# A decoder trunk on one core: loads, remainders and waits reordered at the start, at gate and up, and at the per-layer gate

## The reference

```
h = rmsnorm(x, norm_mix[i]);  proj = h @ w_in            # the indexer's columns first, in layer 0
x = x + mixer(proj) @ w_out[i]
h = rmsnorm(x, norm_ffn[i])
x = x + (gelu(dwconv(h @ w_gate[i])) * (h @ w_up[i])) @ w_down[i]
gate = sigmoid(rmsnorm(x, norm_ple[i]) @ w_ple_gate[i])
x = x + gate * (p[i] @ w_ple_proj[i])
```

## Time and profile before

| | |
|---|---|
| median of 3 runs | 3091.38 us (3091.03 to 3097.04) |
| the profiled execution | 3092.02 us, its span 3090.1 us |
| mean granted TensorE clock | 0.991 |
| PE busy | 2984.3 us, 97% of the span, 14830 matmuls |
| PE busy, tenths of the first four of 40 slices (77 us each) | 7, 9, 9, 9 |
| DVE, ACT, POOL busy | 73%, 47%, 34% |
| DMA | 349.07 MB moved, mean 113 GB/s |

### The profile page before, as it was taken

One profiled execution on the slowest core, in us unless ns is written; L12 is line 12 of the kernel. 1 busy time (PEld: TensorE's weight loads), 2 busy tenths in 40 slices (PEclk: granted clock), 3 DMA queues, 4 the chain that ended last, 5 costly groups with the idle time before them and its releaser, 6 DMA issues. The chain is left out here.

```text
span 3090.1 us, 44240 instructions
## 1 busy us (share of the span) xinstructions
PE 2984.3 (97%) x14830; PEld 2499.8 (81%) x14830; DVE 2255.3 (73%) x3681; ACT 1443.5 (47%) x3127; POOL 1059.7 (34%) x689
## 2 busy tenths in 40 slices
PE   7999999999999999999989999999999999999989
PEld 6778887988878888888868888899887888888867
DVE  5599987889378888888743341899548888879852
ACT  4385536878243334344522211888534333344531
POOL 3105445465223323201122645677323333310120
PEclk9999999999999999999999999999999999999999
DMA  5323334222314563476211694333122222276411
GB/s 175 128 58 99 96 127 108 50 56 68 130 61 150 157 157 101 147 248 194 79 48 41 215 199 147 87 68 75 48 90 72 82 82 82 82 261 216 136 48 48
DMA packets 288086, 349.07 MB, mean 113 GB/s; under 512 B 88316, under 2 KB 181292, under 8 KB 287916
## 3 DMA queue, kind: packets, MB, share of 16 engines
...
...
## 5 line engine op out<-in xcount | busy, mean ns | idle before, releaser
L2188 DVE TENSOR_SCALAR_CACHE_REDUCE k_x<-k_x,l0in_cand,l0in_want 128x384 bf16<-128x384 f32 (+1 forms) x186 | 175.0, 1004 | 1.2 <-DVE l0in_before L2183 0.2
L78 PE MATMUL l1in_acc<-k_w_lo,k_hi 128*128 128x512 f32 x384 | 151.0, 393 | 4.2 <-PEq L99 2.4
L80 PE MATMUL l1in_acc<-k_w_hi,k_hi 128*128 128x512 f32 x384 | 150.0, 391 | 0.0
L79 PE MATMUL l1in_acc<-k_w_hi,k_lo 128*128 128x512 f32 x384 | 149.9, 390 | 0.0
L2567 ACT ACTIVATE k_x<-k_x 128x512 f32<-128x512 f32 x88 | 55.6, 632 | 185.6 <-DVE k_x L2773 180.9
L725 DVE TENSOR_TENSOR l1in_sq<-l1in_out 128x512 f32<-128x512 f32 x32 | 41.3, 1291 | 111.4 <-ACT l1in_out L658 110.6
L1649 DVE TENSOR_TENSOR l1dil_pt_lo<-l1dil_ring,l1dil_pt_hi 128x512 fp32r<-128x512 f32 x192 | 101.9, 553 | 4.6 <-ACT l1dil_pt_hi L1585 2.3
L1585 ACT ACTIVATE l1dil_pt_hi<-l1dil_ring 128x512 fp32r<-128x512 f32 x192 | 92.4, 492 | 22.7 <-PE l1dil_ring L1732 21.4
L1665 DVE CUSTOM_DVE_ANT_0 l1dil_s<-l1dil_s,l1mix_sliding 128x128 f32<-128x128 f32 (+7 forms) x128 | 97.2, 761 | 7.4 <-PE l1dil_s L1749 2.2
L2665 POOL TENSOR_TENSOR l1ff_raw_g<-l1ff_raw_g 128x512 f32<-128x512 f32 x10 | 12.9, 1291 | 243.4 <-DVE l1ff_w_lo L2729 243.4
L2665 POOL TENSOR_TENSOR l0ff_raw_g<-l0ff_raw_g 128x512 f32<-128x512 f32 x10 | 12.9, 1292 | 231.2 <-DVE l0ff_w_lo L2729 231.2
...
## 6 DMA issues: line engine op xcount, KB each, us to landing
...
k_raw<-in_w_in_odd SPq DMA_DIRECT2D x24, 512.0 KB, 4.9
...
```

The costliest lines, as they stand in the source:

```text
L78: pe.matmul(out, a_hi, b_lo, start=start, stop=False)
L79: pe.matmul(out, a_lo, b_hi, start=False, stop=False)
L80: return pe.matmul(out, a_hi, b_hi, start=False, stop=stop)
L2188: tick(dve.tensor_scalar(hits[:, cols], score[:, cols], cand[:, i:i + 1].bitcast(F32), want[:, i:i + 1], ALU.is_ge, ALU.add, accum_out=exc ...
```

## The change

In the first stage, chunks 2 and 3 get a buffer of their own, `early`, laid over a part of `w_lo` that is written only later (second strip); so four chunks are in flight. The norm weights are copied second instead of third. The four remainders of the first strip are made by DVE and no longer by POOL, which waits for them before its later work. ACT takes the squares of tile 1 behind `split(1)`, and `round(1)` and the squares of tile 2 behind `split(3)`. PE turns tile 1 in the middle of unit 0. In the per-layer gate, `p`'s second half is issued behind the second chunk instead of behind the fifth. In gate and up, PE's steps of the first three pieces wait for nothing (POOL gave them their counts before), tile 7 is scaled between the two sums, POOL's first addition waits until it is scaled, and piece 5 is split and finished before the second sums.

```diff
+        early_in = [st.sem(f"early_in{b}") for b in range(2)]
+        early = st.sb("early", [P, 2 * kc, 512], at=low_at + KD * 512 * 4)
...
             def load(n):
                 s, c = n // CH, n % CH
-                if n >= 2:
-                    sp.wait_ge(lo_ready, n - 1)
+                if n >= 4:
+                    sp.wait_ge(lo_ready, n - 1 if n >= 6 else n - 3)
...
             load_x(0)
+            feed.load(sp)
             sp.dma_start(square[:], square_src).then_inc(square_in, 16)
-            feed.load(sp)
             load(0)
+            load(1)
             load_x(1)
-            load(1)
+            load(2)
+            load(3)
             for t in range(2, 4):
                 load_x(t)
...
             square(0)
-            square(1)
             split(0)
             feed.round(act, 0)
             split(1)
+            square(1)
+            split(2)
+            split(3)
+            feed.round(act, 1)
             square(2)
-            split(2)
-            feed.round(act, 1)
-            split(3)
             square(3)
...
-            feed.root(pool, 0)
-            feed.root(pool, 1)
-            low(0)
-            low(1)
-            feed.root(pool, 2)
-            low(2)
-            low(3)
+            for t in range(3):
+                feed.root(pool, t)
+            pool.wait_ge(lo_ready, CH)
...
             scale(0)
+            low(0)
+            feed.rest(dve, 0)
+            low(1)
             scale(1)
-            feed.rest(dve, 0)
+            low(2)
+            low(3)
+            feed.rest(dve, 1)
             scale(2)
-            feed.rest(dve, 1)
...
             feed.turn(pe, 0)
-            feed.turn(pe, 1)
...
+                    if u == 0 and k == KD // 2:
+                        feed.turn(pe, 1)
@@ ple_stage, SP
                 buf.load(sp, n, raw_in[n % 2])
-            sp.wait_ge(p_turned, 2)
-            buf.load_p(sp, 1, p_arrived)
+                if n == CH + 1:
+                    sp.wait_ge(p_turned, 2)
+                    buf.load_p(sp, 1, p_arrived)
@@ ffn_stage
             copy_sum(0, 1)
+            split(5)
             second_high(1)
-            split(5)
...
-            pool.sem_inc(w_lo_done[0], 2)
-            pool.sem_inc(w_lo_done[1], 1)
             pool.sem_inc(w_sum, 4)
             feed.prepare(pool)
             feed.root(pool, LAST)
+            pool.wait_ge(feed.scaled, 1)
             add_weights(0, 6, 0)
...
-            sums_of(LAST - 2, LAST)
+            sums_of(LAST - 2, LAST, 0)
             feed.scale(dve, LAST)
+            sums_of(LAST - 2, LAST, 1)
             low(3)
...
+            low(5)
             dve.wait_ge(feed.rested, 1)
             dve.wait_ge(feed.summed, 1)
             sums_of(LAST, NT)
-            low(5)
             second_low(1)
...
-                pe.wait_ge(w_lo_done[m], q // 2 + 1)
+                if q >= buf.BEGUN:
+                    pe.wait_ge(w_lo_done[m], q // 2 + 1 - READY[m])
```

More of the change, by code:

```diff
@@ L257, in index_projection_stage @@
         w_hi = st.sb("w_hi", [P, 2, KD, 512], F32R)
+        low_at = nc.sbuf_base - Stage.zone
         w_lo = st.sb("w_lo", [P, 2, KD, 512], F32R)
@@ L290, in load @@
                 s, c = n // CH, n % CH
[L291 to L294 removed]
+                if n >= 4:
+                    sp.wait_ge(lo_ready, n - 1 if n >= 6 else n - 3)
+                sp.dma_start(cell(n), sources[s][c * kc * P:(c + 1) * kc * P, :]
+                             .rearrange("(k p) n -> p k n", p=P)).then_inc((early_in if n in (2, 3) else raw_in)[n % 2], 16)
             def load_x(t):
@@ L309, in _ @@
                     sp.dma_start(angle[:, i, :, :], rope[i, :, 0:HALF].rearrange("(t p) c -> p t c", p=P)).then_inc(angle_in, 16)
-            load(2)
-            load_x(4)
-            load(3)
-            for t in range(5, NT):
+            for t in range(4, NT):
                 load_x(t)
@@ L344, in split @@
             def split(n):
-                act.wait_ge(raw_in[n % 2], 16 * (n // 2 + 1))
+                if n in (2, 3):
+                    act.wait_ge(early_in[n % 2], 16)
+                else:
+                    act.wait_ge(raw_in[n % 2], 16 * (n // 2 + (n < 2)))
                 if n == 2 * CH:
                     act.wait_ge(filled, NT)
-                act.activation(halves_of[n // CH][0][:, n % CH * kc:(n % CH + 1) * kc, :], raw[:, n % 2, :, :], ACT.Copy).then_inc(hi_ready, 1)
+                act.activation(halves_of[n // CH][0][:, n % CH * kc:(n % CH + 1) * kc, :], cell(n), ACT.Copy).then_inc(hi_ready, 1)
             def split_queries(u):
@@ L2859, in down_slot, with sums_of @@
                     nfeed.rest(dve, (k - 8) // 2)
-            def sums_of(t, end):
+            def sums_of(t, end, half=None):
                 at = slice((t - NT // 2) * P, (end - NT // 2) * P)
@@ L2865, in sums_of @@
                 n = 2 * (t == LAST)
-                dve.tensor_tensor(b12[:, :, at], b22[:, :, at], b12[:, :, at], ALU.subtract).then_inc(t_sum, 1)
+                if half != 1:
+                    dve.tensor_tensor(b12[:, :, at], b22[:, :, at], b12[:, :, at], ALU.subtract).then_inc(t_sum, 1)
+                if half == 0:
+                    return
                 dve.wait_ge(t_sum, n + 1)
```

20 lines of the change are left out of this document (14 added, 6 removed).

## The result

The changed kernel takes 3071.42 us, the median of 4 runs (3067.17 to 3073.45), against 3091.2 us for the kernel before, timed beside it (4 runs, 3089.97 to 3097.04). The ratio is 0.9929, with a 95% interval of 0.9916 to 0.9943: 22 us less by the ratio, 19.8 by the medians. The forecast was 3069 us (3062.5 to 3078). The profiled execution took 3071.02 us, its span 3068.9, 21.2 us less than the span before; its mean granted clock was 0.994, against 0.991. PE is busy for 2981.5 us, 97% of the span, and its first of 40 slices has 8 tenths instead of 7.

The account below looks back on a forecast made before the run. PE, busy in 97% of the span, was taken as the bound, its waits as the possible gain. Terms -5.3 - 8.8 - 10.2 + 1.8 = -22.5 took the profiled 3092.02 to 3069.5, given as 3069 us (3062.5 to 3078).

Parts of the forecast that it names:

- First stage: Start of the kernel: tile 2's turn starts near 24.1 instead of 29.4, -5.3 us, with -3.5 as lower end.
- After the change chunk 0 still lands when it did: First stage: chunk 0's copy still lands at 10.9, since only copies already ahead of it are ahead of it.
- 3.8 us ... plus 0.4: First stage, PE: unit 0's twelve matmuls take 3.8 us as before, plus 0.4, ending at 18.9.
- Per-layer gates: Both layers: early `p` removes its wait, unit 1's sigmoid is late next; -8.8 us in layer 0, -10.2 in layer 1.
- The parts without the clock: Per-layer gates: unit 3 starts sooner by 7.7 us in layer 0 and 7.9 in layer 1, without clock gains.
- the shorter gaps ... leave it at 2.4 GHz: Per-layer gates: after gaps of 4.1 and 2.1 us PE's clock stays high, returning 1.1 and 2.3 us.
- so it doesn't move: Per-layer gate: the third chunk waits for POOL's first remainder, not for `p`, so its time stays the same.
- Entries: Entry to gate and up: step 13 comes later, +0.9 us in each layer, +1.8; bounds -1.5 to +2 each.
- 1.70 apiece: Entry to gate and up: piece 5 and two second sums on DVE alternate with POOL's, 1.70 us each, ending at 904.4.
- the two-us delay of the first rounding: Entry to gate and up: the first second_high starts near 892.7, two us later, behind the delayed sum.
- less comes back: Rival: the start keeps only 3.5 us, the clock falls in both gaps, entries cost 2 each; -15, 3077 us; chance 0.17.
- The rival in which the sigmoid is no bound: Rival, per-layer gates: the sigmoid doesn't bind and the entries gain; -34, or half as likely -28, 3058 to 3064; chance 0.15.

Follow-up runs that it names:

- e2: Kernel before with only the early issue of the second half of `p` in the per-layer gate; ratio 0.9953 to the kernel before.
- e3: Kernel before with only the reordered entry to gate and up; ratio 1.0004 to the kernel before.
- e8: Changed kernel with the norm weights' copy back in third place, ahead of chunk 0; one execution, 3079.36 us.
- e9: Changed kernel with the four remainders of strip 0 back on POOL; one execution, 3073.53 us.
- e5: The changed kernel itself, run again; ratio 0.9936 to the kernel before.
- e7: Changed kernel with the old entry to gate and up, and unit 1's sigmoid ahead of the third chunk's split; ratio 0.9888 to the kernel before, 3059.66 us.
- e6: Changed kernel with the entry to gate and up as it was before; ratio 0.9925 to the kernel before.
- e4: Changed kernel with ACT's sigmoid of unit 1 ahead of the third chunk's split in the per-layer gate; ratio 0.9906 to the kernel before.
- e10: e4 with DVE's delayed sum put back whole ahead of tile 7's scale; ratio 0.9904 to the kernel before, 3063.32 us.
- e11: e7 with the entry's changed counts, so PE's first steps don't wait for POOL, no instruction moved; ratio 0.9899 to the kernel before, 3061.55 us.
- e12: e7 run again unchanged; ratio 0.9895 to the kernel before, 3061.59 us.

## Why the prediction was right

**First stage: forecast -5.3, measured -6.4 (-5.6 to -7.0 in the other traces with DVE).** The chain was the one described: chunk 0, rounding, remainder, unit 0; twelve matmuls, turn, twelve matmuls; then the wait for tile 2's scale (1.34 us). One step was mis-sized: "After the change chunk 0 still lands when it did ... 10.9". It landed at 9.35. The reading of the rows was right: with the old order of copies it landed at 10.9, 10.8 and 10.3 us (before, e2, e3). What failed is the premise, "only copies that were ahead of it are ahead of it": in the ten traces with the new order it landed at 9.1 to 9.6. In e8 the copies ahead of chunk 0 are those of the kernel before, in their order, and it landed at 9.69, so the set ahead of it does not decide the time alone; what else does stays open. A second term was too small: the "3.8 us ... plus 0.4" for twelve matmuls and a wait came to 4.94 (12.91 to 17.85), since PE now works through more of the slow first stretch (0.43 us a matmul until 17.4, before until 21.3). The bound "-6.8, if the scale were no bound" was nearly reached with the scale still a bound, since all of it came sooner. The pieces of 1.28 on DVE were right (1.23).

**Per-layer gates: forecast -8.8 and -10.2.** The order of events was right in both layers: `p` off the path, unit 1's sigmoid behind the third chunk's split, 4.5 and 2.4 us left of the 4.1 and 2.1 forecast. The parts without the clock, -7.7 and -7.9, stand against 7.2 and 10.3 in the changed kernel's trace and 6.5 to 7.7 in all others but e9's layer 0 (5.6). What failed is "the shorter gaps ... leave it at 2.4 GHz", worth 3.4 us of the forecast gain: in layer 0 it never did, in layer 1 once in six. In layer 0 of the changed kernel 7.7 + 1.1 - 1.7 for the new low stretch gives 7.1, and 7.2 was measured. The profiled execution was the one in six for layer 1, and that is luck: its total hides the error.

The forecast's "so it doesn't move" for the third chunk held in that one trace and failed in the other five, in layer 1. Unit 3 starts 23.12 us behind the gate's first matmul in the changed kernel's trace and 24.0 to 24.4 in the other five, so of the 2.5 to 2.8 us by which it is ahead of them 0.9 to 1.3 are not the clock. SP issues that chunk when POOL has its first remainder. The rows of POOL and DVE, first of the changed kernel, then of e5:

```profile
2962.59 5.71 POOL L1184 TENSOR_TENSOR l1pg_x_lo<-l1pg_raw,l1pg_x_hi 128x1024 fp32r<-128x1024 f32 x2
...
2962.74 3.31 DVE L175 SCALAR_TENSOR_TENSOR l1pg_xn<-k_x,l1pg_rstd,l1pg_gain 128x1024 f32<-128x1024 f32 x1
```

```profile
2967.73 1.28 DVE L175 SCALAR_TENSOR_TENSOR l1pg_xn<-k_x,l1pg_rstd,l1pg_gain 128x1024 f32<-128x1024 f32 x1
...
2968.17 5.42 POOL L1184 TENSOR_TENSOR l1pg_x_lo<-l1pg_raw,l1pg_x_hi 128x1024 fp32r<-128x1024 f32 x2
```

Where POOL started 0.15 us ahead of DVE, the first of its two remainders took 2.4 us and the copy was issued 17.24 us behind the gate's first matmul (17.26 in the kernel before); where DVE was ahead, the remainder took 3.1 and the copy was issued at 18.16. POOL was first in the kernel before, in the changed kernel and in e7, DVE in the other eleven traces. The wait that is left ahead of unit 3 in layer 1 follows from it: 2.4 us in the changed kernel, 3.7 in e5, e8 and e9, and 2.0 in e2 and e6, where a low stretch between the two gaps held PE up. So the forecast's 2.1 was met by an outcome that did not repeat. With the sigmoid first (e4, e7, e10, e11, e12) layer 0 gave 12.3 to 12.7, layer 1 11.7 to 13.0, near the -13.0 and -12.5 that the forecast had for a sigmoid at no cost.

**Entries: forecast +0.9 each, measured +0.3 and +0.2 at step 13, +0.5 each in e3.** The chain through ACT's split of piece 8 and DVE's wait was right and half the size: the three DVE operations at "1.70 apiece" took 1.37, 1.77 and 1.65 us. The forecast set the two-us delay of the first rounding at its head; e10 shows that it has no part in it. The later start of the second sums, which it also had, is what is left.

**The sum.** -6.4 - 7.2 - 10.3 + 0.5 = -23.4 for what the change touches, +2.4 from stages it does not touch, -21 in all. As means over all traces that have the part (nine, six, six, seven), its terms come to -6.1, -6.6, -8.1 and +0.9 (48.31 us to step 13 with the changed entry, 47.88 without, in two layers), that is -19.9 us, beside the 19.8 of the medians. The nearer of the two rivals on this side was "less comes back" (3077): its clock part was true, its start was not. The rival in which the sigmoid is no bound gave 3058 to 3064, and e7 shows that it was one line of ACT's list away.
